# Two early half units, zero products and a later first score in a fused transformer kernel on one core

## The reference, cut to what matters

```python
ada = silu(c) @ w_ada[l] + b_ada[l]          # c: (1, 1024), six vectors of 1024: shift, scale, gate, shift, scale, gate
h   = x * (1 + scale) + shift                # feature by feature
qa, ka, va, qb, kb, vb = split(h @ w_in_ab)  # 1024 -> 3072
oa = differential attention (4 heads, two softmax maps each, T5 bias), then RMS norm per head
ob = dilated attention (8 heads, T5 bias)
y  = concat(oa, ob) @ w_o                    # then gate, residual, layer norm, SwiGLU FFN ("ff0"), next layer "cd"
```

## Time and profile before

| what | value |
|---|---|
| time, median of 3 runs | 1677.32 us (1677.19 to 1680.98) |
| the profiled execution | 1675.25 us, span 1673.4 us, mean granted clock 0.992 |
| PE busy | 1613.1 us, 96% of the span |
| DVE, ACT busy | 1086.2 us (65%), 804.9 us (48%) |
| first weight product on PE | 44.27 us after the span's start |
| first score | 58.77 us |

### The profile page before, as it was taken

How to read it: one execution, slowest core, us unless ns; L and a number is a source line. 1 busy time by engine, 2 the same in 40 slices (tenths; PEclk the granted TensorE clock), 3 DMA queues, 4 the chain that set the end, 5 groups by cost and what they waited for, 6 DMA issues and landing times.

```text
span 1673.4 us, 24653 instructions
## 1 busy us (share of the span) xinstructions
PE 1613.1 (96%) x9268; PEld 1346.8 (80%) x9268; DVE 1086.2 (65%) x1332; ACT 804.9 (48%) x1033; POOL 224.4 (13%) x300
## 2 busy tenths in 40 slices
PE   3999999999999999999999999999999999999999
PEld 2997788778887888778888978888888889878887
DVE  7798877877759456765546886554555546765544
ACT  1565533336555444554346756444454345664443
POOL 2101001000000000078926200000000002200000
PEclk9999999999999999999999999999999999999999
DMA  9976787884644755465554425656466555445652
GB/s 321 334 252 203 280 293 278 280 297 127 218 148 148 271 197 178 148 190 186 189 176 151 153 89 173 199 177 198 153 202 197 179 196 161 138 160 178 198 178 99
DMA packets 225750, 330.10 MB, mean 197 GB/s; under 512 B 10423, under 2 KB 187160, under 8 KB 225678
## 3 DMA queue, kind: packets, MB, share of 16 engines
q1 hardware_dynamic: 210480, 276.93, 50.7%
q0 software_dynamic: 14800, 52.06, 9.0%
q10 hardware_dynamic: 398, 0.11, 0.0%
HBM read 327.97 MB, written 1.09 MB: 197 GB/s over the span
## 4 chain that ended last, share of the span: by engine, by line
PE 75%; DVE 12%; DMA 7%; ACT 3%; issue 2%; SPq 0%; POOLq 0%; DVEq 0%; POOL 0%; ACTq 0%
PE bank L2797 35%; PE bank L2539 22%; PE bank L2527 7%; DMA s_late<-in_w_ada 5%; DVE s_late L1924 4%; PE bank L2497 3%; DVE s_wL L1899 2%; PE bank L2809 1%; DMA s_mix<-in_w_ada 1%; PE bank L2509 1%; ACT s_wH L1459 1%; DVE s_late L1936 1%; DMA s_raw<-in_w_ffn_in 1%; PE bank L2638 1%; PE bank L2594 1%
## 5 line engine op out<-in xcount | busy, mean ns | idle before, releaser
L1899 DVE TENSOR_TENSOR s_wL<-s_raw,s_wH 128x2048 fp32r<-128x2048 f32 x251 | 581.2, 2316 | 292.2 <-ACT s_wH L1459 291.8
L1459 ACT ACTIVATE s_wH<-s_raw 128x2048 fp32r<-128x2048 f32 x254 | 485.3, 1911 | 232.0 <-PE bank L2797 139.9
L2797 PE MATMUL bank<-s_wH,s_hH 128*128 128x512 f32 x1056 | 420.9, 399 | 5.8 <-DVE s_hL L2261 3.3
L2797 PE MATMUL bank<-s_wH,s_hL 128*128 128x512 f32 x1056 | 412.6, 391 | 0.0
L2797 PE MATMUL bank<-s_wL,s_hH 128*128 128x512 f32 x1056 | 412.0, 390 | 0.0
L2797 PEld LDWEIGHTS bank<-s_wH,s_hH 128*128 128x128 f32 x1056 | 198.7, 188 | 50.6 <-issue 9.1
L2797 PEld LDWEIGHTS bank<-s_wH,s_hL 128*128 128x128 f32 x1056 | 198.5, 188 | 42.7
L2797 PEld LDWEIGHTS bank<-s_wL,s_hH 128*128 128x128 f32 x1056 | 199.0, 188 | 39.8 <-issue 0.7
L2539 PE MATMUL bank<-s_wH,s_aH 128*128 128x512 f32 x496 | 195.0, 393 | 1.1 <-DVE s_hL L2028 0.9
L2539 PE MATMUL bank<-s_wH,s_aL 128*128 128x512 f32 x496 | 193.9, 391 | 0.0
L2539 PE MATMUL bank<-s_wL,s_aH 128*128 128x512 f32 x496 | 193.7, 390 | 0.0
(11 more groups left out here) (454 smaller groups left out, 2249.3 us busy)
## 6 DMA issues: line engine op xcount, KB each, us to landing
s_raw<-in_w_ffn_in SPq DMA_DIRECT2D x88, 512.0 KB, 4.9
s_raw<-in_ffn_w_gate SPq DMA_DIRECT2D x88, 512.0 KB, 3.9
s_raw<-in_ffn_w_up SPq DMA_DIRECT2D x88, 512.0 KB, 4.9
s_raw<-in_ffn_w_down SPq DMA_DIRECT2D x88, 512.0 KB, 4.2
s_late<-in_w_ada POOLq DMA_DIRECT2D x20, 2048.0 KB, 10.3
s_raw<-in_w_ffn_out SPq DMA_DIRECT2D x44, 512.0 KB, 4.9
s_raw<-in_w_in_ab SPq DMA_DIRECT2D x24, 512.0 KB, 9.3
s_raw<-in_w_in_cd SPq DMA_DIRECT2D x24, 512.0 KB, 4.7
```

The costliest lines, as they stand in the source:

```text
L1459: A(wH[:, slot, :], raw[:, slot, :], ACT.Copy).then_inc(hi_ready, 1)
L1899: TTn(wL[:, slot, :], raw[:, slot, :], wH[:, slot, :].bitcast(F32), ALU.subtract).then_inc(lo_ready, 1)
L2797: last = mm(bank[GU_BANK[tt]][:], h, w[:, k, :], start=(half == 0 and k == 0 and i == 0), stop=(half == 1 and k == 3 and i == 2), skip_gro ...
```

## The change: what it does

1. **Order of the blocks.** `FIRST_COLS` = (0, 2, 1, 3): the first half of shift and the first half of scale are summed first, then the second halves. The fourth block is loaded into the area of the first one, so SP waits for DVE's eight sums of the first block before it issues that load.
2. **x by halves.** Two DMAs of 512 KB (features 0 to 511, 512 to 1023), and eight transposes after each (`turn_columns`). Of the four banks, the third is now bank 1 instead of bank 6.
3. **Units 0 to 2 by halves of the inner index.** SP issues the first halves (k 0 to 3) among the setup loads, the second halves after ACT has rounded the first three. ACT and DVE split by halves (`split_half`). PE runs 24 matmuls for each first half (`half_unit(u, 0)`) as soon as k 0 to 3 of h exist, then the second transposes and sums, then `half_unit(0, 1)` and `half_unit(1, 1)`, then `dense(32, 44)`.
4. **Zeros.** `keep_busy(0, 14)` after the third block's PE sum, `keep_busy(0, 10)` after the fourth's.
5. **Modulation by halves** (`modulated(half)`) on ACT and DVE.
6. **LEAD** is 44 in this mixer instead of 36. The other mixer (cd) keeps 36.
7. **ADA_STEPS** of this mixer: the pieces of the first two blocks are taken one step later (steps 2 to 5 instead of 1 to 5), and the PE sum and the evacuation of the first one move from steps 3 and 4 to 4 and 5.
8. POOL's load of the bias waits for the fourth block too. Some semaphores are merged (sub_part).

```diff
-                      (mix[:, 0:2048], mix[:, 2048:4096]), (t32[:].rearrange("p k t -> p (k t)"), mix[:, 4096:6144]))]
+                      (mix[:, 0:2048], mix[:, 2048:4096]), (ada_raw[:, 0, 0:2048], ada_raw[:, 0, 2048:4096]))]
+        FIRST_COLS = (0, 2, 1, 3)
...
-        LEAD, STEPS = 36, 13
+        EARLY = 3
+        LEAD, STEPS = (44, 36), 13
...
-        ADA_STEPS = ({1: [(1, 2, 0, 4)], 2: [(1, 2, 4, 8)], 3: [(0, 2, 0, 3)], 4: [(0, 2, 3, 6)], 5: [(0, 2, 6, 8), (1, 3, 0, 1)],
-                      6: [(1, 3, 1, 5)], 7: [(1, 3, 5, 8)], 8: [(0, 3, 0, 3)], 9: [(0, 3, 3, 6)], 10: [(0, 3, 6, 8)],
+        ADA_STEPS = ({2: [(1, 2, 0, 4)], 3: [(1, 2, 4, 8)], 4: [(0, 2, 0, 4)], 5: [(0, 2, 4, 8)],
+                      6: [(1, 3, 0, 5)], 7: [(1, 3, 5, 8)], 8: [(0, 3, 0, 3)], 9: [(0, 3, 3, 6)], 10: [(0, 3, 6, 8)],
...
@@ queue of SP
             first_ada(0)
             first_ada(1)
-            sp.dma_start(x[:], a["x"][0].rearrange("(a p) d -> p a d", p=P)).then_inc(ev("x_in"), 16)
+            sp.dma_start(x[:, :, 0:512], x_in[:, :, 0:512]).then_inc(ev("x_in0"), 16)
+            half_unit(0, 0, ab_units[0])
+            half_unit(1, 0, ab_units[1])
             first_ada(2)
+            half_unit(2, 0, ab_units[2])
+            sp.dma_start(x[:, :, 512:D], x_in[:, :, 512:D]).then_inc(ev("x_in1"), 16)
+            sp.wait_ge(ada_step[0], 8)
             first_ada(3)
-            qkv("ab", a["w_in_ab"][0])
+            sp.wait_ge(ev("first_hi"), EARLY)
+            for u in range(EARLY):
+                half_unit(u, 1, ab_units[u])
+            straight("ab", ab_units, EARLY)
...
@@ queue of ACT
             first_ada(0)
+            split_half(0, 0)
             first_ada(1)
+            modulated(0)
+            split_half(1, 0)
+            split_half(2, 0)
+            first_ada(2)
+            split_half(0, 1)
             first_ada(3)
+            modulated(1)
+            split_half(1, 1)
+            split_half(2, 1)
...
@@ queue of DVE
+            def modulated(half):
+                r, g = TR["ab"], 2 * half
+                dve.wait_ge(ada_out[0], half + 2)
+                dve.wait_ge(ada_out[1], half + 2)
+                sc = adaC[:, 0, 8 + 4 * half:12 + 4 * half]
+                step(TS(sc, sc, 1.0, None, ALU.add))
+                dve.sem_inc(ev("scale_ready"), 1)
+                dve.wait_ge(tr_done, TRD["ab"] + g + 1)
+                for c in (2 * g, 2 * g + 1):
+                    last = TS(t32[:, c, :], bank[TURN_BANK["ab"][g]][:, (c % 2) * T:(c % 2) * T + T], adaC[:, 0, 8 + c:9 + c],
+                              adaC[:, 0, c:c + 1], ALU.mult, ALU.add)
+                last.then_inc(t32_ready, 1)
+                if half == 0:
+                    split_half(0, 0)
+                lower_part(r, g)
+                lower_part(r, g + 1)
+                split_half(1, half)
...
@@ queue of PE
+                if l == 0:
+                    for u in range(3):
+                        half_unit(u, 0)
+                    pe.wait_ge(ev("toep_rows"), 1)
+                    turn_columns(1)
+                    ada(0, 0, 1, False)
+                    pe.wait_ge(ada_out[0], 3)
+                    keep_busy(0, 14)
+                    ada(0, 1, 1, False)
+                    keep_busy(0, 10)
+                    half_unit(0, 1)
+                    pe.wait_ge(ev("lam_part"), 3)
+                    mm(bank[1][:, 384:385], ones[0:1, :], lam[0:1, 5:6], start=True, stop=True).then_inc(ev("lam_part"), 1)
+                    half_unit(1, 1)
+                else:
+                    dense(0, 16)
...
-                dense(16, LEAD)
+                dense(16 if l else 32, LEAD[l])
```

More of the change, by code:

```diff
@@ L1195, in qkv, with straight @@
                                  col_unit(w, m * 1536 + j * 256 + 512 * u))
-            def straight(name, units):
-                for u, src in enumerate(units):
+            def straight(name, units, first=0):
+                for u, src in enumerate(units[first:], first):
                     n = START[name] + u
@@ L2325, in _ @@
                 .then_inc(ev("dt_rows"), 1)
-            ada(0, 1, 2)
+            modulated(0)
             dve.wait_ge(ev("toep_mm"), 1)
@@ L2596, in turn_tile, with turn_columns @@
                         last.then_inc(tr_done, 1)
+            def turn_columns(half):
+                pe.wait_ge(ev(f"x_in{half}"), 16)
+                for tt in range(TT):
+                    for k in range(KC // 2 * half, KC // 2 * half + KC // 2):
+                        at = (k % 2) * T + tt * P
+                        last = pe.transpose(bank[TURN_BANK["ab"][k // 2]][:, at:at + P], x[:, tt, k * P:k * P + P], ident[:])
+                        if tt and k % 2:
+                            last.then_inc(tr_done, 1)
             def transposed(name):
                 busy = BUSY[name] if name in BUSY else (0, 0)
-                if name in ("ab", "cd"):
+                if name == "cd":
                     keep_busy(TURN_BANK[name][0], busy[0])
@@ L2733, in ada_turn, with half_unit @@
                     ada(l, slot, cnt, slot == 0, b)
-                dense(0, 16)
+                def half_unit(u, half):
+                    if half:
+                        pe.wait_ge(lo_ready, u + (LO0 + 1))
+                    else:
+                        pe.wait_ge(ev("first_lo"), u + 1)
+                    H, L = (w[:, u, :].rearrange("p (k c) -> p k c", k=KC) for w in (wH, wL))
+                    for pair in (2 * half, 2 * half + 1):
+                        if u == 0:
+                            pe.wait_ge(tl_ready, 4 * TR["ab"] + pair + 1)
+                        for half_at in range(2):
+                            for k in (2 * pair, 2 * pair + 1):
+                                cut = slice(half_at * P, half_at * P + P)
+                                if u == 2:
+                                    products = ((hH[:, k, cut], H[:, k, :]), (hH[:, k, cut], L[:, k, :]), (hL[:, k, cut], H[:, k, :]))
+                                else:
+                                    products = ((H[:, k, cut], hH[:, k, :]), (H[:, k, cut], hL[:, k, :]), (L[:, k, cut], hH[:, k, :]))
+                                for i, (w, z) in enumerate(products):
+                                    last = mm(bank[4 + u][:, half_at * T:half_at * T + T], w, z, start=(half_at == 0 and k == 0 and i == 0),
+                                              stop=(k == KC - 1 and i == 2), skip_group_check=True)
+                    if half:
+                        last.then_inc(unit_used, 1)
+                if l == 0:
[12 more added lines that the diff above has]
+                    half_unit(1, 1)
+                else:
+                    dense(0, 16)
                 if l == 1:
@@ L2752, in mixer @@
                         turn_o(1)
-                    dense(LEAD + 12 * s, LEAD + 12 * s + 12)
+                    dense(LEAD[l] + 12 * s, LEAD[l] + 12 * s + 12)
                     if l == 1 and s == 5:
@@ L2960, in _ @@
             pe.transpose(bank[2][:, 128:176], rowC, ident[0:48, 0:48]).then_inc(ev("cols_tr"), 1)
-            pe.wait_ge(ev("x_in"), 16)
-            transposed("ab")
-            ada(0, 0, 1, False)
-            ada(0, 1, 1, False)
-            pe.wait_ge(ev("lam_part"), 3)
-            mm(bank[1][:, 384:385], ones[0:1, :], lam[0:1, 5:6], start=True, stop=True).then_inc(ev("lam_part"), 1)
-            pe.wait_ge(ada_out[0], 3)
             for l, (p, o, f) in enumerate((("ab", "o_ab", "ff0"), ("cd", "o_cd", "ff1"))):
```

67 lines of the change are left out of this document (38 added, 29 removed).

## The result

The changed kernel takes 1688.51 us (median of 4 runs, 1687.52 to 1691.05) against 1677.8 us before (4 runs on the same chip): the ratio is 1.0069 with a 95% interval of 1.0057 to 1.0081, slower by more than the 0.3% that can be told from no change. I had forecast 1680.8 us with a range of 1674 to 1687. The sign of the sum was right and its size was not: +10.7 us in place of +3.5. The profiled execution of the changed kernel is the longest of its four, 1691.05 us, 15.8 more than the profiled one of before. On a second chip the same kernel measured 1.0074 (1.0059 to 1.0090).

A forecast was written before the change was run, and what follows sets the result against it. Three limits: setup by DVE, dense products by PE, mixer's tail by DVE. The first score's +3.5 us, unchanged through the sixth score and tail, added to 1677.3 gave 1680.8 us, range 1674 to 1687.

The forecast's parts named there:

- fourth block's end: Setup on DVE: the fourth block's sums end at 45.4 us, after the modulation and third block placed ahead of them.
- second halves: End of setup: PE's products of the units' second halves can start at 51.9 us, bounds 50.6 to 58.6.
- zeros at full clock behind the third sum: Setup on PE: fourteen zero products of 0.21 us each, 3.0 us, hold back the fourth sum by 2.6 us.
- first score: Start of attention: 28 entries of 0.36 us after the second halves start, at 62.2 against 58.77 us, +3.5.
- unit 2's early half lost: Early products on PE: bank 6 is begun again, so only 48 of 72 early matmuls count; PE stream 0.7 us later.
- nothing given back by the tail: Sixth score to out_half: DVE and ACT have the same work, 24.35 us, so out_half moves from 138.75 to 142.2.
- Rivals A: Setup on PE: zero and half products run at half clock, up to 6.7 us on top, 1684 to 1688; chance 0.16.
- C: Mixer's tail: DVE and ACT catch up 2.9 us, so not slower, 1676.7 to 1678 us; chance 0.15.
- D: Setup and tail: second halves at about 46.5 with a PE-bound tail, faster beyond 0.3%, 1671.4 us; chance 0.08.
- Rival B: Loads of units 3 to 6 arrive late beside POOL's loads: +1.5 to 3 us, 1682.5 to 1684; chance 0.10.
- From first to sixth score it is PE's chain of the same work as before, 55.63 us: Attention's first scores: PE's stretch keeps its length of 55.63 us, putting the sixth score at 117.8.
- I carry the shift of 138.75 through to the end: After the mixer's out_half: later work hangs on the tail in unchanged order, so the +3.5 us stays to the end.

The follow-up runs named there:

- first repair: Changed kernel plus one wait: POOL issues its first 2 MB load of w_ada only when unit 5 has landed; 1680.57 us, ratio 1.0040.
- reverse experiment: Kernel before plus one wait: SP asks for unit 5 only when PE has used unit 1; 1680.77 us, ratio 1.0024.
- both repairs: Two separate edits of the changed kernel: POOL waits for unit 5 (1680.57 us), or POOL's first load early and its second behind unit 5 (1680.76 us).
- two variants of the kernel before: Kernel before with only unit 5 asked for late (ratio 1.0024), and with only LEAD 44 and the new ada steps (1.0011).
- kernel at 0.9985: Changed kernel with early load, unit 2's half kept, LEAD 40, no zeros before fourth sum, third sum and column tables moved; 1671.7 us, ratio 0.9985.
- early-load kernel: Changed kernel with POOL's first w_ada load moved into the DMA hole and the second behind unit 5; 1680.76 us, ratio 1.0051.
- first four variants: Changed kernel with, one each: POOL waiting for unit 5 (1.0040), POOL's first load early (1.0051), LEAD 36 (1.0092), unit 2's early half kept (1.0077).
- four kernels with both repairs: Changed kernel with early load and unit 2's half kept (1.0016); also LEAD 40, no fourth-sum zeros (0.9986); also two pieces moved (0.9985); that with LEAD 44 (0.9987).
- first one with LEAD 40: Changed kernel with early load, unit 2's early half kept, LEAD 40 and no zeros ahead of the fourth sum; 1674.27 us, ratio 0.9986.

## Why the prediction was wrong

**Right.** First product at 27.43 (28.0), fourth block's end at 44.5 (45.4), second halves at 51.79 (51.9), zeros at full clock behind the third sum, first score at 62.6 (62.2), unit 2's early half lost, nothing given back by the tail: out_half came 24.3 to 24.4 us after the sixth score in all thirteen profiles, whatever had been edited. Rivals A, C and D did not occur. Rival B did: ACT waited 7.63 us for s_raw, and PE stood still between 64 and 90, at its turn.

**The step that failed** is the sentence "From first to sixth score it is PE's chain of the same work as before, 55.63 us", and with it the price of rival B: "up to 6 us of delay less 4.6 of slack", +1.5 to 3 us at a chance of 0.10. Three things were wrong in it.
- The delay. I moved the request of a unit later and left its landing time alone. But the request moved onto POOL's two loads, which the setup had not moved away by as much: 17.25 us to landing for its second half, where it took 12.1 before and 6.1 once POOL waited, and 8.9 us later than before. The price stood in the trace that I had: unit 6 took 17.0 us beside the same two loads. Nor were the DMA engines "full before", as rival B has it.
- The queue behind it. I had named DVE's maxima as what could double the price, and did not follow them: ACT, DVE's split, the maxima of pair 1, both splits of unit 6 and PE's turn stand one behind the other, so the stall ended at 86.7, not when unit 5 was needed.
- The clock. The wait of 3.55 us was followed by products at half clock, 0.7 on the scores and 1.6 on 36 products; the price had no such term, although shows the same dip twice.

Sum for 62.60 to 124.99: 3.55 idle, 2.4 of clock, 0.6 on the turn (0.90 for 0.33), together 6.5 of the measured 6.8. The first repair takes it back with one wait (66.5 us from T2 to the sixth score in place of 73.2), the reverse experiment puts a late unit 5 into the old kernel and gets the same picture. That the late request is harmless by itself is shown too: both repairs leave it where it was and only clear the way for it.

Two slips in the sums changed nothing: DVE's first modulation would start at 24.7 by its own terms, not 24.85, and rival D's second halves at 46.9, not 46.5.

**What the change is worth without the accident**: +7.3 and +7.4 us (the two repairs, by the medians; their profiles have +4.9 and +3.1 at the sixth score), against my +3.5. A second step of the prediction failed here: "I carry the shift of 138.75 through to the end". It does not stay what it is. I set every profile against that of before, instruction by instruction on DVE:

- From the sixth score to 300 us the shift falls by 1.1 to 3.4 us in the ten profiles with the new setup, and by 0.2 and 0.8 in the two variants of the kernel before. In `ff0` PE waits for DVE four times before, 2.4 us in all (at 202, 221, 239 and 293 us), 2.1 in the old setup with LEAD 44, and not at all with either repair. Why is open. The kernel at 0.9985 is 0.5 us ahead of before at the sixth score of its profile, 2.9 ahead at 300 us and 4.6 at the end, so most of its gain lies outside the edited stretch, and its cause isn't shown.
- At 447 us PE waits for DVE, and DVE for a load of `w_ada`. In the seven profiles in which this load took 8.5 to 9.1 us PE waited 1.1 to 1.7 us; in the six in which it took 9.5 to 10.5, PE waited 2.1 to 3.1 and then ran at half clock for 5 us or more.

So it is in part luck that the +10.6 us of the changed kernel at the sixth score equal the +10.7 of its medians: in its profile the shift goes to +9.5 at 300 us and ends at +15.8. The early-load kernel, chain and windows at 447 us:

```profile
431.41 10.18 DMA s_late<-in_w_ada
```

```profile
442.50:447.30 4.80, 2.07 (x18) 1.86 (x16) 4.73 (x9) 2.40 (x2) 0.00 (x0) 0.95 0.03 11
447.30:450.40 3.10, 3.07 (x12) 2.31 (x12) 3.03 (x4) 0.87 (x2) 0.00 (x0) 0.50 0.92 325
450.40:454.00 3.60, 3.60 (x19) 2.95 (x19) 3.20 (x11) 1.25 (x6) 0.00 (x0) 0.54 0.34 97
```

The shift grows by 3.5 to 5.7 us between 427 and 467 us in these six, and by 0.1 us at most in the others (two lose 0.3 and 0.5). It was there in both profiles of the changed kernel and in its first four variants, and absent from before, its two variants and the four kernels with both repairs. Why the load took longer in those six stays open: the shift at that point does not decide it (+0.3 us with the dip in the early-load kernel, +0.4 without it in the first one with LEAD 40), and no run took this place alone.

## What to carry to other kernels

When a request moves later, don't keep its landing time: list every transfer asked for within the time it takes to land, add their bytes, look at the size of their packets, and look for the hole in front in which one of them could have gone. The trace of before can hold the price already, on the neighbour that meets the same traffic. When a wait appears, price it as wait plus what is queued behind the waiting instructions plus the products at half clock after it. Work done early is worth something only if the code that follows continues it; here two thirds counted, and the last third only once the data were in time.

## What the runs showed of the hardware

- A stall of 3.6 us in the middle of dense work cost 2.4 us more in clock. In layer 1 waits of 1.1 to 1.7 us left the clock at 1.00 in seven profiles, and waits of 2.1 to 3.1 were followed by 0.50 in six. The length of one wait doesn't decide it everywhere: in the kernel before, waits of 0.24, 1.36 and 0.86 us stood ahead of the 0.50 at 139.6.
- How long the clock stays down after the same setup differs between executions: the products that began at 44.3 and 44.7 us, behind the same idle stretch, ran at 0.50 for 3 us in one and 6 us in the other, 1.4 us of difference with no edit behind it. Profiles of single executions differ by as much; hence +4.8 in the profile and +1.7 in the medians for LEAD 44.
- The second half of a unit (512 KB, asked for just behind the first) landed 4.5 to 4.7 us after its issue when nothing else was moved (unit 4 in the changed kernel and in the first repair), 6.1 to 6.4 behind other units alone (unit 5 with either repair and with both), 12.1 and 12.2 when POOL's loads met a part of it (unit 5 before, and late in the kernel before), and 17.0 to 18.3 beside two loads of 2 MB (unit 6 before; unit 5 in the changed kernel twice, with LEAD 36, and with unit 2's half kept).
- It does not get half of the rate. The DMA queues while both have work, in the changed kernel from 60 to 70 us and in the kernel before from 58 to 70 (packets, MB, share of the engines' time):

```profile
q0 software_dynamic: 782, 3.01, 79.4%
q1 hardware_dynamic: 783, 0.79, 23.6%
```

```profile
q0 software_dynamic: 925, 3.57, 78.5%
q1 hardware_dynamic: 937, 0.94, 24.1%
```

The two queues move the same number of packets, and POOL's (q0) are larger: 3.85 KB in the mean against 1.0 KB of SP's (q1), by division. So POOL gets 3.01 MB where SP gets 0.79, a fifth, at 382 GB/s together. By this rate POOL's 4.2 MB hold up SP's queue for 14 us, during which it moves 1.1 MB, about one unit: an estimate that fits the landings at 17.25 and 17.0 us. The Trainium skill, "DMA: Bandwidth & Descriptors", section "Queues, rings and completion order", says that a DMA engine takes turns between its queues packet by packet. The trace agrees: 782 to 783 here, and 783 to 779 with LEAD 36 (62 to 72 us); whether the profile counts the same packets as the page, no run shows. No run changed the size of the packets, so that smaller ones of POOL's would have brought unit 5 in earlier is not shown.
